# A two-layer mixer step on one core: only the first layer's shift and scale ahead of the tokens, the other modulation rows by VectorE in the merge

## The chip, the core and the metric

The kernel runs on one core of one Trainium2 chip. The metric is the device time of one launch in microseconds (us), lower is better. Engines are named as the profile names them: PE is TensorE (PEld its weight loads), DVE is VectorE, ACT is ScalarE, POOL is GpSimd, SP is SyncE. ACTq, DVEq and SPq are the sequencers of these engines; a DMA is issued from one of them.

## The reference, cut to what matters

Two layers, 1,152 tokens (1,024 latent, 128 context), model width 1,024, float32. What the change touches is the modulation:

```python
for l in range(DEPTH):                                   # DEPTH = 2
    mod = jax.nn.silu(cond) @ ada_w[l] + ada_b[l]        # (1024) @ (1024, 3072), for c and for c_ctx
    shift, scale, gate = jnp.split(mod, 3, axis=-1)
    h = rms_norm(x, norm_g) * (1.0 + scale) + shift      # needed at the start of the layer
    ...                                                  # h @ w_in, three branches
    merged = g0 * (y_a @ w_br_a) + g1 * (y_b @ w_br_b) + g2 * (y_c @ w_br_c)
    x = x + gate * (merged @ w_out)                      # gate is needed at the end of the layer
```

Latent tokens are modulated by `c`, context tokens by `c_ctx`, so each modulation row of 128 channels has two columns.

## The kernel before, in words

Channels lie on the 128 partitions: 1,024 channels are KD = 8 slices k, tokens are the free axis, cut in NT = 3 tiles of 384 columns. Every engine has a program of its own, written out by hand, and semaphores join them; no scheduler reorders anything. A projection (`product`, `tile`, `project`, L336 to L355) multiplies each float32 weight block of 128x1024 as three products (high by high, low by high, high by low), so one block over the three tiles is 8 x 3 x 3 = 72 matmuls. The result tiles rotate over PSUM banks 0, 1 and 2 (`take`, L328): a tile waits until the tile three places earlier has been read out. SP loads the weight blocks into two slots (L670, L672), POOL splits each into high and low (L686, L688) once PE is done with the block two places earlier.

**Prologue.** ACT issues `par`, `sq_c`, `mask_in`, the whole of `X` (L694 to L697) and six of the sixteen slabs of `ada_w` (L735; one slab is 128 input channels of one layer by all 3,072 outputs). ACT squares the 8 slices of X (L709) and DVE adds them up (`norm_add`, L1224, L1226), in turns through two buffers. PE sums over the partitions (`norm_sum`, L374, L377), ACT makes 1/rms (`root`, L701, L703) and then `cond` = SiLU of c (L727). Then PE makes the modulation of both layers: for each of the 16 slabs six matmuls with `cond` as the stationary operand and 512 columns moving (L393), 96 a layer; ACT copies the finished 2x3072 row block (L733, L738), PE turns it by 24 small transposes (L400), and DVE adds the bias and forms `mod` and `amul` (L1273 to L1279). ACT still works out two exponentials (L741, L743), DVE the small constants behind them (L1247 to L1268).

**First normalised slices.** For each k, DVE scales X by 1/rms into `n_t` (L1289), ACT applies scale and shift (L752) and rounds to `h_hi` (L757), DVE forms the remainder `h_lo` (L1295). PE runs the first projection slice by slice behind them (`project_as_split`, L357).

**Merge and output.** A layer ends with three merges, one a branch, of 8 rows j. For each j PE projects G(j) (72 matmuls) and Y(j) (36 matmuls); ACT takes the sigmoid of the three tiles of G (`merge`, L1127), DVE multiplies them with the tiles of Y (L1588) and adds them to X (L1592). Then come the loads of `x_res` (L1198), the split of X (L1201, L1635), and the output projection, whose read-out uses the gate rows of `mod` (L1646). Layer 1 starts with another `norm_sum`.

```python
for l in range(DEPTH):          # PE, prologue
    for k in range(KD):
        for n in range(6):
            mm = pe.matmul(ps[0:2, n, :], cond[:, k, :], slabs[:, s % 6, n * 512:(n + 1) * 512], ...)
```

## Time and profile before

| | us |
|---|---|
| median of 3 runs (3261.82 to 3265.61) | 3263.72 |
| the profiled execution, whole | 3263.88 |
| its span in the profile | 3262.0 |
| PE busy | 3102.9 (95%) |
| DVE busy | 1341.8 (41%) |
| ACT busy | 1073.5 (33%) |
| POOL busy | 696.4 (21%) |

The profile is of one execution. Its span runs from the first to the last instruction that it shows; the execution took 1.9 us more. The chain of waits is followed back from the last instruction, at each step to what released it; its pieces have a start, a length and a name. In a timeline a row is a start, a busy time and an instruction, "x4" after it means four instructions merged in that row, and the bracket at its end is the idle time before it and who ended it. A group of matmuls is pipelined: the ends are modelled, so starts are what is compared.

### The profile page before, as it was taken

Reading aid. Unit: us, or ns where it says so; the run is one execution under the profiler, and the core shown is the slowest. Engines: PE = TensorE matmul, PEld = TensorE weight load, DVE = VectorE, ACT = ScalarE, POOL = GpSimd, SP = SyncE. Lnnn points to the kernel's source line nnn. Section 1 sums busy time; section 2 is a strip of 40 time slices with the busy share of each in tenths; the row PEclk is TensorE's granted clock in tenths of the full one; section 3 lists DMA queues with packets and bytes.
Section 4 is the critical chain, followed back from the end, with each engine's and each line's share of the span. In section 5 each row is a group of like instructions: output and inputs, shape, how many; then the busy total and the mean of one; then the engine's idle time right before and its main releaser. Section 6 shows DMA issues by size and latency. Waiting matters only on the chain.

```text
span 3262.0 us, 43857 instructions
## 1 busy us (share of the span) xinstructions
PE 3102.9 (95%) x18496; PEld 2953.9 (91%) x18496; DVE 1341.8 (41%) x1777; ACT 1073.5 (33%) x2038; POOL 696.4 (21%) x404
## 2 busy tenths in 40 slices
PE   5799999999999999999988999989999999999999
PEld 1299998889889999999988999988888999999999
DVE  1255666566654111121225566646565421112121
ACT  1234344465554211010114343445565431101010
POOL 0021211111111123333331211211111112233322
PEclk9899999999999999999999999999999999999999
DMA  8310111100011012111330111110000101121131
GB/s 321 142 35 30 41 40 47 33 24 23 30 36 68 24 43 68 46 42 40 135 126 28 36 38 36 34 47 23 30 29 30 68 31 34 48 68 44 44 108 71
DMA packets 52115, 182.58 MB, mean 56 GB/s; under 512 B 5584, under 2 KB 12752, under 8 KB 49232
## 3 DMA queue, kind: packets, MB, share of 16 engines
q1 hardware_dynamic: 28800, 92.29, 9.4%
q10 hardware_dynamic: 23120, 87.49, 7.0%
q8 instruction: 147, 2.41, 0.3%
q14 instruction: 48, 0.39, 0.0%
HBM read 149.35 MB, written 30.41 MB: 55 GB/s over the span
## 4 chain that ended last, share of the span: by engine, by line
PE 88%; DVE 4%; ACT 4%; issue 1%; ACTq 1%; DMA 1%; DVEq 1%
PE ps L339 64%; PE ps L436 4%; PE ps L544 3%; PE ps L393 3%; PE ps L518 2%; PE ps L519 2%; PE ps L531 2%; DVE stat L1502 1%; PE ps L482 1%; PE ps L602 1%; DVE b_qs L1482 1%; PE ps L474 1%; PE ps L604 1%; DVEq L1483 1%; ACT b_eb L1010 1%
## 5 line engine op out<-in xcount | busy, mean ns | idle before, releaser
L339 PE MATMUL ps<-h_hi,w_hi 128*128 128x384 f32 x3648 | 1242.6, 341 | 50.0 <-DVE h_lo L1295 27.3
L339 PE MATMUL ps<-h_hi,w_lo 128*128 128x384 f32 x3648 | 1226.2, 336 | 0.0
L339 PE MATMUL ps<-h_lo,w_hi 128*128 128x384 f32 x3648 | 1226.2, 336 | 0.0
L339 PEld LDWEIGHTS ps<-h_hi,w_hi 128*128 128x128 f32 x3648 | 690.5, 189 | 58.1 <-issue 57.0
L686 POOL CAST w_hi<-w_raw 128x1024 fp32r<-128x1024 f32 x200 | 202.0, 1010 | 2524.0 <-PE ps L339 2519.2
L339 PEld LDWEIGHTS ps<-h_hi,w_lo 128*128 128x128 f32 x3648 | 690.6, 189 | 0.9 <-issue 0.5
L339 PEld LDWEIGHTS ps<-h_lo,w_hi 128*128 128x128 f32 x3648 | 689.7, 189 | 0.0
L688 POOL TENSOR_TENSOR w_lo<-w_raw,w_hi 128x1024 fp32r<-128x1024 f32 x200 | 494.2, 2471 | 16.0
L1127 ACT ACTIVATE m_g<-ps 128x384 f32<-128x384 f32 x144 | 70.7, 492 | 763.7 <-PE ps L339 754.1
L1502 DVE TENSOR_REDUCE stat<-ps 128x1 f32<-128x1152 f32 (+1 forms) x144 | 177.8, 1235 | 237.1 <-PE ps L519 237.1
L1588 DVE TENSOR_TENSOR m_p<-ps,m_g 128x384 f32<-128x384 f32 x96 | 53.5, 558 | 476.4 <-PE ps L339 476.4
L339 PE MATMUL ps<-y_lo,w_hi 128*128 128x384 f32 x576 | 192.4, 334 | 0.0
L339 PE MATMUL ps<-y_hi,w_hi 128*128 128x384 f32 x576 | 192.4, 334 | 0.0
L339 PE MATMUL ps<-y_hi,w_lo 128*128 128x384 f32 x576 | 192.4, 334 | 0.0
L544 PEld LDWEIGHTS ps<-b_wt,b_v 128*128 128x128 f32 x1168 | 138.9, 192 | 33.5 <-ACT b_wt L1017 24.5
L544 PE MATMUL ps<-b_wt,b_v 128*128 128x128 f32 x1168 | 145.1, 277 | 17.4 <-ACT b_wt L1017 17.4
L518 PE MATMUL ps<-b_kh,b_qs 128*128 128x384 f32 (+1 forms) x400 | 146.3, 366 | 14.1 <-ACT b_eb L1010 9.0
L519 PE MATMUL ps<-b_kl,b_qs 128*128 128x384 f32 (+1 forms) x400 | 134.3, 336 | 0.0
L436 PE MATMUL ps<-a_q,a_km 128*128 128x128 f32 x1008 | 132.8, 286 | 0.0
L1588 DVE TENSOR_TENSOR X<-ps,m_g 128x384 f32<-128x384 f32 x48 | 26.8, 557 | 257.5 <-PE ps L339 257.5
L436 PEld LDWEIGHTS ps<-a_q,a_km 128*128 128x128 f32 x1008 | 127.6, 192 | 2.6 <-ACT a_km L821 1.1
L1010 ACT ACTIVATE b_ea<-ps,stat 128x1152 f32<-128x1152 f32 (+1 forms) x72 | 81.3, 1129 | 144.4 <-DVE stat L1502 144.4
(226 smaller groups left out, 3582.9 us busy)
## 6 DMA issues: line engine op xcount, KB each, us to landing
w_raw<-in_w_full SPq DMA_DIRECT2D x152, 512.0 KB, 3.5
ada_slabs<-in_ada_w ACTq DMA_DIRECT2D x16, 1536.0 KB, 7.6
w_raw<-in_w_half SPq DMA_DIRECT2D x48, 256.0 KB, 2.6
x_res<-x_keep ACTq DMA_DIRECT2D x16, 576.0 KB, 8.6
out_x_new<-X ACTq DMA_DIRECT2D x16, 576.0 KB, 2.8
X<-in_x_t ACTq DMA_DIRECT2D x1, 4608.0 KB, 17.8
x_keep<-X ACTq DMA_DIRECT2D x1, 4608.0 KB, 13.3
y_keep<-a_y ACTq DMA_DIRECT2D x8, 576.0 KB, 2.8
```

The source lines that it names most:

```text
L339: mm = pe.matmul(ps[:, bank, 0:TILE], w[:, slot, k, :], r[:, k, cols_of(t)], start=(k == 0 and i == 0), stop=(k == kt - 1 and i == 2))
L393: mm = pe.matmul(ps[0:2, n, :], cond[:, k, :], slabs[:, s % 6, n * 512:(n + 1) * 512], start=(k == 0), stop=(k == KD - 1))
L436: mm = pe.matmul(o, a_km[lev % 2][:, cs], both_ways(a_q2, c, 1 << lev), start=True, stop=True)
L518: pe.matmul(o, b_qs[:, m, i * P:(i + 1) * P], b_kh[:, m, ks], start=True, stop=False)
L519: mm = pe.matmul(o, b_qs[:, m, i * P:(i + 1) * P], b_kl[:, m, ks], start=False, stop=True)
L544: mm = pe.matmul(ps[:, 6 + ring % 2, 0:P], b_v[:, CH if i == CTX else kt, :], b_wt[:, kt, :], start=(kt == 0), stop=(kt == CH - 1 or i == ...
L686: pool.tensor_copy(w_hi[:, slot, 0:kt, :], raw).then_inc(w_hi_done, 1)
L688: pool.tensor_tensor(w_lo[:, slot, 0:kt, :], raw, w_hi[:, slot, 0:kt, :].bitcast(F32), ALU.subtract).then_inc(w_split, 1)
L1010: act.activation(dst, src, ACT.Exp, bias=stat[:, pos % 3, m:m + 1], accum_out=stat[:, pos % 3, 2 + m:3 + m]).then_inc(b_exp, 1)
L1127: act.activation(m_g[:, t, :], seen(l, ("G", br, j), t), ACT.Sigmoid)\
L1502: dve.tensor_reduce(stat[:, pos % 3, m:m + 1], src, AX.X if ctx_block else AX.XY, ALU.max, negate=True).then_inc(b_max, 1)
L1588: dve.tensor_tensor(dst, seen(l, name, t), m_g[:, t, :], ALU.mult).then_inc(free(l, name, t), 1)
```

## The change

The first layer's shift and scale are worked out in four column groups; a group q holds shift rows 2q, 2q+1 and scale rows 2q, 2q+1, so that it completes slices 2q and 2q+1 of the tokens. Its weights come as two halves of 1,024 KB. ACT issues groups 0 and 1, then works out `cond`, then issues the 8 slices of X with a semaphore each, then groups 2 and 3, then the masks. SP holds the first weight block back until the last slice of X has landed. The scaled X is written in place, so DVE no longer waits for ACT's buffers (`first_scaled`, `first_affine`, `first_low`). The store of X into `x_keep` ahead of layer 0 is gone (the residual of layer 0 is read from the input), and layer 0 stores X to `x_keep` alone.

The 32 other rows (8 gate rows of layer 0, all 24 of layer 1) move to the last merge of a layer: 24 in layer 0, 8 in layer 1. ACT loads one row's weights at a time (128x1024, 512 KB, three buffers) and `cond` as 128x2x1024; DVE forms each of the two columns of a row by one `tensor_tensor_reduce` over 1,024 elements, whose product goes to PSUM banks 3 to 6 and whose sum, with the bias as its start value, goes to `mod`. `PHASES` says how many rows are summed ahead of the products of each j.

```diff
+GROUPS = 4
+LATE = ([(0, 2 * KD + j) for j in range(KD)] + [(1, j) for j in range(2 * KD)],
+        [(1, 2 * KD + j) for j in range(KD)])
+PHASES = ((0, 3, 4, 4, 4, 3, 3, 3), (0, 2, 1, 1, 1, 1, 1, 1))
+SLABS = 3
...
         @block.tensor
...
-            pe.wait_ge(const_in, 48)
-            norm_sum(0)
-            pe.wait_ge(n_rs_s, NT)
-            pe.wait_ge(cond_ready, 1)
-            for l in range(DEPTH):
...
+            def modulation_rows(q):
                 for k in range(KD):
+                    if k % 4 == 0:
+                        pe.wait_ge(group_in[2 * q + k // 4], 16)
+                    mm = pe.matmul(ps[0:2, 3 + q, :], cond[:, k, :], groups[q][:, k, :],
+                                   start=(k == 0), stop=(k == KD - 1))
+                mm.then_inc(ada_mm, 1)
...
+            pe.wait_ge(const_in, 32)
+            pe.wait_ge(cond_ready, 1)
+            modulation_rows(0)
+            modulation_rows(1)
+            modulation_turned(0)
+            norm_sum(0)
+            modulation_turned(1)
+            modulation_rows(2)
+            modulation_rows(3)
+            modulation_turned(2)
+            modulation_turned(3)
+            pe.wait_ge(n_rs_s, NT)
...
         @block.sync
         def _(sp):
+            sp.wait_ge(x_in_s[KD - 1], 16)
...
         @block.scalar
...
+            for i in range(GROUPS):
+                group_load(i)
+            act.wait_ge(const_in, 32)
+            act.activation(cond[:, :, :].rearrange("p k c -> p (k c)"), par[:, PC_C:PC_C + 2 * KD],
+                           ACT.Silu).then_inc(cond_ready, 1)
+            for k in range(KD):
+                act.dma_start(X[:, k, :], x_in[:, k, :]).then_inc(x_in_s[k], 16)
+            for i in range(GROUPS, 2 * GROUPS):
+                group_load(i)
+            act.dma_start(mask_in[:, :, :], masks).then_inc(mask_in_s, 16)
...
+            def first_affine():
+                for k in range(KD):
+                    act.wait_ge(n_xr, k + 1)
+                    if k % 2 == 0:
+                        act.wait_ge(mod_ready, k // 2 + 1)
...
+                        if last and j == 0 and t == 0:
+                            act.wait_ge(y_lo_s, l * 12 + 12)
+                            act.dma_start(cond_b[:, :, :], cond_rows).then_inc(cond_in, 16)
+                            late_load(SLABS)
+                        if last and j and t < 2:
+                            late_load(begun + SLABS + min(1 + t, PHASES[l][j]))
...
         @block.vector
...
+            row_kept(0)
+            row_kept(1)
+            modulation(0)
+            dve.wait_ge(n_rs_s, NT)
+            first_scaled(0)
+            first_scaled(1)
+            modulation(1)
+            for k in range(2, KD):
+                first_scaled(k)
+            first_low(0)
+            row_kept(2)
+            first_low(1)
+            row_kept(3)
+            modulation(2)
+            modulation(3)
+            for k in range(2, KD):
+                first_low(k)
...
+            def late_sums(l, j):
...
+                    for c in range(2):
+                        ins = dve.tensor_tensor_reduce(
+                            ps[:, 3 + 2 * c:5 + 2 * c, :], late[n % SLABS][:, :].rearrange("p (b k) -> p b k", b=2),
+                            cond_b[:, c, :].rearrange("p (b k) -> p b k", b=2), 1.0,
+                            par[:, PC_AB + layer * 24 + row:PC_AB + layer * 24 + row + 1],
+                            ALU.mult, ALU.add, mod[:, layer, row, c:c + 1])
+                    ins.then_inc(late_used, 1)
...
             def merge(l, order, br):
                 for j in range(KD):
+                    if order == len(BRANCHES) - 1:
+                        late_sums(l, j)
                     dve.wait_ge(m_gate, l * 24 + order * 8 + j + 1)
```

`row_kept(q)` is DVE's copy of a finished 2x512 row block out of PSUM, `modulation(q)` three small DVE operations that make the shift and scale of two slices.

PE's program at the start, of before (L374 and L377 are `norm_sum`, L393 the modulation matmuls, L400 the transposes, L339 the first projection):

```order
L374 MATMUL ps<-n_acc,sq_c 128x384 [waits n_added,const_in]
L377 MATMUL ps<-n_sq,sq_c 128x384 [waits n_squares]
L393 MATMUL ps<-ada_slabs,cond 2x512 [waits slab_in0,cond_ready,n_rstd]
L400 MATMUL ps<-sq_c,mod_row 128x2 [waits ada_row]
L393 MATMUL ps<-ada_slabs,cond 2x512 [waits slab_in2,ada_row]
L400 MATMUL ps<-sq_c,mod_row 128x2 [waits setup_done,ada_row]
L339 MATMUL ps<-h_hi,w_hi 128x384 [waits n_lo,n_hi,w_split]
```

and of the change (L404 the modulation matmuls of a group, L411 its transposes, L394 and L397 `norm_sum`, L358 the projection):

```order
L404 MATMUL ps<-ada_group_136,cond 2x512 [waits group_in0,cond_ready,const_in]
L404 MATMUL ps<-ada_group_137,cond 2x512 [waits group_in2]
L411 MATMUL ps<-sq_c,mod_row 128x2 [waits ada_row]
L394 MATMUL ps<-n_acc,sq_c 128x384 [waits n_added]
L397 MATMUL ps<-n_sq,sq_c 128x384 [waits n_squares]
L404 MATMUL ps<-ada_group_138,cond 2x512 [waits group_in4]
L404 MATMUL ps<-ada_group_139,cond 2x512 [waits group_in6]
L358 MATMUL ps<-h_hi,w_hi 128x384 [waits n_hi,n_lo,w_split,n_rstd]
```

The two full blocks of modulation matmuls between the norm's sums and the projection are replaced by four groups, two of them ahead of the sums; one set of transposes stands ahead of `norm_sum`, one behind it and two ahead of the projection.

DVE's program between the norm's sums and the last slice, of the change (L1339 is `row_kept`, L1347 to L1351 `modulation`, L1355 `first_scaled`, L1359 `first_low`):

```order
L1293 TENSOR_TENSOR n_acc<-n_acc,n_sq 128x1152 [waits n_squares] x6
L1339 COPY mod_row<-ps 2x512 [waits ada_mm] x2
L1347 TENSOR_TENSOR amul<-ps,scale_b 128x4 [waits ada_t]
L1355 TENSOR_TENSOR X<-X,n_rs 128x1152 [waits n_rstd]
L1355 TENSOR_TENSOR X<-X,n_rs 128x1152 x6
L1359 TENSOR_TENSOR h_lo<-X,h_hi 128x1152 [waits n_hi]
L1339 COPY mod_row<-ps 2x512 [waits ada_mm]
L1351 TENSOR_TENSOR amul<-amul,par 128x4
L1359 TENSOR_TENSOR h_lo<-X,h_hi 128x1152 [waits n_hi] x6
```

Before, DVE took one scaling and one remainder in turn for each slice; now all eight scalings stand ahead of the first remainder, and the scale and shift of slices 4 to 7 behind two remainders.

DVE's program in the last merge, of the change (L1719 and L1723 are the products and the sum of the merge, L1687 the product that completes SiLU, L1696 the two instructions of one `tensor_tensor_reduce`):

```order
L1723 TENSOR_TENSOR X<-X,m_p 128x1152
L1687 TENSOR_TENSOR cond_b<-cond_b,ps 128x2048 [waits cond_sigmoid]
L1696 ISA ps,mod<-ada_late_146,cond_b,par 128x1024 [waits late_in0]
L1696 ISA mod 128x1
L1719 TENSOR_TENSOR m_p<-ps,m_g 128x384 [waits tile_done1,m_gates]
```

The sums stand between the end of one j and the first product of the next; each is a long instruction and a short one that writes the accumulated value.

## Rows read from the trace of the kernel before

**Rows 1.** The page: busy time of the engines, and the ended-last chain by engine.

```profile
PE 3102.9 (95%) x18496; PEld 2953.9 (91%) x18496; DVE 1341.8 (41%) x1777; ACT 1073.5 (33%) x2038; POOL 696.4 (21%) x404
...
PE 88%; DVE 4%; ACT 4%; issue 1%; ACTq 1%; DMA 1%; DVEq 1%
```

**Rows 2.** The chain of waits from 0 to 175 us: start, length, what.

```profile
2.13 17.84 DMA X<-in_x_t
...
21.34 2.22 ACT n_sq L709 x2
...
32.34 4.18 PE ps L374 x6
...
42.01 0.53 ACT n_rs L703
...
44.16 43.34 PE ps L393 x96
...
158.12 1.24 ACT n_h L752
...
163.69 1.24 ACT n_h L752
...
170.87 0.78 PE ps L339 x3
```

**Rows 3.** DMA, 0 to 230 us: rate in 40 slices; issues (KB, us to landing).

```profile
GB/s 222 444 438 413 427 425 430 197 0 274 299 291 306 314 321 312 75 216 310 21 0 3 0 151 412 259 1 0 0 0 51 66 0 91 3 91 0 90 4 0
...
X<-in_x_t ACTq DMA_DIRECT2D x1, 4608.0 KB, 17.8
...
sq_c<-in_squares ACTq DMA_DIRECT2D x1, 256.0 KB, 6.1
```

**Rows 4.** Timeline of the prologue: single operations of ACT and DVE.

```profile
1.65 0.45 ACTq L696 DMA_DIRECT2D mask_in<-in_masks  x1
...
20.04 1.28 ACT L709 ACT_TABLE_LOAD   x1 [20.04 <-DMA X<-in_x_t]
...
144.48 0.21 DVE L1273 TENSOR_TENSOR mod<-ps,par 128x48 f32<-128x48 f32 x1 [2.35 <-PE ps L400]
...
145.28 2.62 DVE L1289 TENSOR_TENSOR n_t<-X,n_rs 128x1152 f32<-128x1152 f32 x2
```

**Rows 5.** Timeline of PE at the first slices: two starts, and two more later.

```profile
152.18 0.52 PE L339 MATMUL ps<-h_hi,w_hi 128*128 128x384 f32 x1
...
152.50 0.52 PE L339 MATMUL ps<-h_hi,w_lo 128*128 128x384 f32 x1
...
157.22 0.33 PE L339 MATMUL ps<-h_hi,w_lo 128*128 128x384 f32 x1
...
157.39 0.33 PE L339 MATMUL ps<-h_lo,w_hi 128*128 128x384 f32 x1
```

**Rows 6.** Timeline of DVE in the last merge of layer 0.

```profile
1452.97 0.56 DVE L1588 TENSOR_TENSOR m_p<-ps,m_g 128x384 f32<-128x384 f32 x1 [6.43 <-PE ps L339]
...
1457.71 1.36 DVE L1592 TENSOR_TENSOR X<-X,m_p 128x1152 f32<-128x1152 f32 x1
1471.69 0.56 DVE L1588 TENSOR_TENSOR m_p<-ps,m_g 128x384 f32<-128x384 f32 x1 [12.61 <-PE ps L339]
...
1475.78 0.56 DVE L1588 TENSOR_TENSOR m_p<-ps,m_g 128x384 f32<-128x384 f32 x1 [1.52 <-PE ps L339]
```

**Rows 7.** Timeline of POOL there: the remainder of a full and of a half block.

```profile
1470.76 2.40 POOL L688 TENSOR_TENSOR w_lo<-w_raw,w_hi 128x1024 fp32r<-128x1024 f32 x1
...
1476.57 2.37 POOL L688 TENSOR_TENSOR w_lo<-w_raw,w_hi 128x512 fp32r<-128x512 f32 x1
```

**Rows 8.** Single lines of DVE: duration ns min/median/max, first and last start.

```profile
L1461 DVE TENSOR_TENSOR b_q<-b_qn,b_rope x8: 1224/1225/1226, 560.7 to 2421.3; 128x1024 f32<-128x1024 f32 x8
...
L1313 DVE SCALAR_TENSOR_TENSOR a_f<-a_f,oml,lbv x8: 1409/1414/3549, 188.7 to 2018.5; 128x1152 f32<-128x1152 f32 x8
```

**Rows 9.** Groups of DVE by line and shape: busy us, mean ns, idle before.

```profile
L1470 DVE TENSOR_TENSOR b_kt<-ps,b_rope 128x512 f32<-128x512 f32 x16 | 10.4, 683 | 8.6 <-PE ps L482 8.6
```

204 lines of the change are left out of this document (130 added, 74 removed).

## The prediction

> **What bounds the kernel now.** I read the page first: PE is busy for 95% of the span, and 88% of the chain that ended last is PE [rows 1]. So a change pays only where PE works on something avoidable, or waits. Next I read the chain of waits over the first 175 us [rows 2], since the change works there. X lands at 2.13 + 17.84 = 19.97; squares and their sums take from 21.34 until `norm_sum` starts at 32.34; 1/rms ends at 42.54; then come two blocks of 96 modulation matmuls, the first of 43.34 us. Only at 170.87 does PE start the last slice of the first projection; from there the program is the same in both kernels until the last merge. This instant is my yardstick for the front. The reader should see that some 87 us of modulation are PE work in the chain that nothing else covers, and that the rest of the front is hand-over between DMA, ACT and DVE. Last I read one row j of the last merge of layer 0 [rows 6, 7], since the displaced work goes there.
>
> **The front, step by step (times in the new kernel).** It loses 192 matmuls and 48 transposes and gets 32 matmuls and 16 transposes; I follow the new chain.
>
> 1. `sq_c` lands 6.1 us after its issue near 1.2 [rows 3], so the constants are there at 7.3 and `cond` (a 128x16 activation, 0.2) at 7.5. ACT then issues 13 DMAs (8 of X, 4 half groups, the masks) at 0.45 each [rows 4]: 13.4. A table load of 1.28 [rows 4] and two tiny exponentials: about 15.1.
> 2. Is X there? Ahead of its slice 0 stand 0.6 MB of constants and 4.2 MB of groups; with slice 0 it is 5.4 MB, with all of X (4,608 KB, [rows 3]) 9.5 MB. The slices of the rate are 5.75 us long; summed up they move 5.4 MB by 15.1 and 9.5 MB by 24.9 [rows 3]. Before, X itself was complete when 7.5 MB had moved, about 0.8 MB more than stood up to its end, because later transfers share. I add 1.2 us for that: slice 0 at 16.3, slice 6 at 24.7, slice 7 at 26.1.
> 3. From the first square to the start of `norm_sum` it took 32.34 - 21.34 = 11.0 [rows 2]. From 16.3 that gives 27.3, and slice 6 with its square (1.16) and its sum (1.36) gives 27.2: both limits agree. DVE's dozen small constants of 0.2 each [rows 4] are done by 17.5, beside the first two squares.
> 4. New in the chain: PE turns group 0 ahead of `norm_sum`, and this waits for DVE's copy `row_kept(0)`, which in program order stands behind the sums. A read of 512 PSUM columns is 0.68 [rows 9], four transposes with hand-overs 0.5: 28.5. `norm_sum` to 1/rms takes 42.54 - 32.34 = 10.2 as before [rows 2]: 38.7. Groups 0 and 1 are done long before (16 matmuls from 7.5, under 1 us each); groups 2 and 3 run behind `norm_sum`, beside ACT's and DVE's work.
> 5. From 38.7 two chains race. ACT starts slice 0 after the first scaling (1.36), at 40.1, and takes (163.69 - 158.12) / 2 = 2.79 a slice [rows 2]; it wants shift and scale of slice 4 at 51.2. DVE first has eight scalings and two remainders at 1.31 (two took 2.62 [rows 4]), 13.1; two row copies at 0.68; `modulation(1)` and `(2)` at 0.8 each (from 144.48 to 145.28 [rows 4]): 16.1 in all, 54.8. **So ACT stalls for 3.6 us at slice 4**: that is what is late next in the front.
> 6. ACT takes slices 4 and 5 in 5.6, and from the start of slice 6 to PE's last slice it is 170.87 - 163.69 = 7.2 [rows 2]: 67.6. PE leaves its last transposes at about 55 with most slices waiting: nine matmuls each, 0.32 apart at the low clock level (1.2 GHz) and 0.17 apart at the high one [rows 5]. It starts low after idling, as before, so 2.9 + 6 x 1.55 bring it to about 67 too. Both meet at slice 7.
>
> Gain of the front: 170.87 - 67.6 = **103.3 us**. The weight blocks, held back until slice 7 of X, are loaded and split (3.5 us each) by about 40: hidden until 55. The dropped store of X ahead of layer 0 and the 8 dropped stores to the output ran beside PE: nothing.
>
> **The merge.** A row j lasts 1471.69 - 1452.97 = 18.7 us of PE. DVE is free from 1459.1, when its sum ends, to 1471.69, the next product: 12.6 us. PE is held only if Y(j, 0) has not been read when G(j+1, 0) wants its bank, 4.1 us later (where the third product starts, 1475.78) [rows 6]. So the room is 16 us. One sum is a DVE pass over two SBUF operands of 1,024 float32 and a short instruction; no row shows this operation. The nearest row, same operands and length, has 1.23; the longest two-operand pass has 3.55 [rows 8]. These are my bounds; I take 1.4, near the first, for the short instruction on top. Four rows of weights a j: 11.2 us. Beside it, POOL: the remainder of a half block takes 2.37, that of a full one 2.40 [rows 7], and the half one began while DVE's sum was running: it waited. I add 1.0 for DVE waiting in turn: 12.2 of 16 us, **hidden**. j = 1 has three rows and the SiLU product of 2,048 columns (2.4): 11.8, hidden. If the cover is gone, PE waits by what exceeds 16. POOL's next full split has PE's 6.2 us of Y(j) for its 3.5. ACT's new issues and waits stand behind its sigmoids, whose banks are wanted 8 us later. The 13.6 MB of new loads over 150 us are 91 GB/s, a fifth of what the prologue's stream reached. Layer 1 has one or two rows a j. I put the merge at 0, up to 3 us in this case.
>
> The Trainium skill (SBUF — State Buffer, "Who interferes with whom") has a VectorE instruction with two SBUF inputs and a GpSimd one that reads SBUF block each other for the whole instruction. By that rule the trace agrees: POOL's 2.37 us for half a block and DVE's 3.55 against a median of 1.41.
>
> **Sum.** 3263.88 (the profiled execution) - 103.3 = 3160.6. That execution lies 0.16 above the median of the runs, so I predict **3160.4 us**. For this case alone 3155 to 3166: below, X without the 1.2 us and less stall at slice 4; above, later transfers and the merge's 3 us.
>
> **Rivals.**
> - *The sums run at half rate.* At 1.2 ns an element [rows 8] doubled, 1,024 take 2.4 us. A row j lasts 1.0 + 2n x 2.4 + 3.3 (three products, sum, gaps): 23.5 for n = 4, +4.8 in three rows; 21.1 at j = 1 with the SiLU product, +2.4; n = 3 just fits. In all +17: 3177. Against: L1313 with two SBUF operands takes 1.41 for 1,152 elements [rows 8]. For: the new instruction also accumulates, and no row does. 12%. The Trainium skill (Vector Engine (DVE) Microarchitecture Reference, "Points that are easy to get wrong") states that a scalar-tensor-tensor form with two SBUF sources other than bf16 halves throughput; the row of L1313 does not show it.
> - *Each sum takes 3.5 us*, held or slow [rows 8]. n = 4: 32.3 a row, +13.6 three times; n = 3: +6.6 three times; j = 1 +9; layer 1 +2. In all +72: 3232. Against: POOL reads for 5 of 18.7 us, mostly at the row's end. 8%.
> - *Slower than before.* The same place further on: by this formula 48 sums in layer 0 and j = 1 of layer 1 stretch the merges by 52c - 110.5 for a price c, which eats 103.3 at c = 4.1 us. At 4.3 the time is 3273. No pass of this size takes that long in the trace. 2%.
> - *The front gains less.* The transfers run at 300 GB/s, as those of the later slabs did [rows 3]: slice 6 lands at 31.8 and the sums end 7 us later, 3167. Or PE stays at the low level through the first eight slices, 8 x 2.9 from 55: +9, 3169. Against: the later slabs were issued one at a time, and PE rose after 3 us before. 10%.
> - *The displaced rows stay in the prologue too* would take the gain; PE's program excludes it, with 32 modulation matmuls in all.
>
> **How the numbers follow.** Forecast 68%, half rate 12%, front less 10%, 3.5 us 8%, slower 2%. The range holds the forecast, the smaller front and the half rate: 3155 to 3177. About 0.2% (6.5 us) is what a measurement of this kernel can tell from no change. All cases but the last are faster by far more: faster 97%, same 1% (a price just above 4), slower 2%.
>
> **What would show it.** In the profile of the changed kernel: the first `n_sq` near 16, the last `n_acc` ending near 27, 1/rms near 39, ACT idle for some 3 us ahead of slice 4, PE's last slice near 67.6, no idle PE in the last merges, a sum near 1.4, products of Y right behind PE. Wrong would be: a sum above 2.0 us (PE then waits for DVE in three rows), a first square after 20, or PE waiting for `w_hi` or `w_lo` in the merge.

## The result and the profile after

| | before | after |
|---|---|---|
| median of the runs | 3264.66 (4 runs, 3261.82 to 3266.22) | 3162.8 (4 runs, 3159.06 to 3165.62) |
| profiled execution, whole | 3263.88 | 3163.95 |
| its span | 3262.0 | 3161.9 |
| start of PE's last slice of the first projection | 170.87 | 71.60 |
| the rest of the span from there | 3091.1 | 3090.3 |

The ratio is 0.969 (95% interval 0.9676 to 0.9705), 101.9 us between the medians. 3160.4 had been forecast, with 3155 to 3177 as the range. Of the 99.9 us between the profiled executions, 99.3 lie ahead of the start of PE's last slice. The rest of the kernel, with the 64 sums in its merges, lasts as long as before.

The page of the changed kernel, against [rows 1]: PE has 59 us less to do, and its share of the chain stays 88%; ACTq has gone from 1% to 2%.

```profile
PE 3043.5 (96%) x18336; PEld 2941.6 (93%) x18336; DVE 1440.4 (46%) x1920; ACT 1069.6 (34%) x2036; POOL 698.7 (22%) x404
...
PE 88%; DVE 4%; ACT 3%; ACTq 2%; issue 1%; DVEq 1%; DMA 0%
```

PE loses 59.4 us of work, but the front loses 99. Before, 102.7 us passed from the end of 1/rms (42.54) to DVE's first scaling (145.28): 86.3 in the two blocks of modulation matmuls (43.34 and 43.00), and 16.4 in the copies, the small transposes, the exponentials and the small constants around them. Now the first scaling follows 1/rms at once (44.12), since the 28 us of modulation matmuls that are left stand beside other work, half while X lands and half beside 1/rms and the first slices. Of the 102.7 us, 1.6 are given back because 1/rms ends later (44.10), and 1.9 because it now takes 27.5 us from the first scaling to PE's last slice where it took 25.6. That leaves the 99.3.

The front of the changed kernel, timeline of ACT (start, busy time, what; the bracket is the idle time before and who ended it), against [rows 2, 4]:

```profile
1.62 1.94 ACTq L725 DMA_DIRECT2D ada_group<-in_ada_first  x4
4.52 0.98 ACTq L733 DMA_DIRECT2D X<-in_x_t  x2
5.53 6.28 ACTq L733 DMA_DIRECT2D X<-in_x_t  x6
11.84 7.01 ACTq L725 DMA_DIRECT2D ada_group<-in_ada_first  x4
18.88 1.20 ACTq L736 DMA_DIRECT2D mask_in<-in_masks  x1
...
21.40 0.22 ACT L760 ACTIVATE lbt<-lbt 128x16 f32<-128x16 f32 x1
21.62 2.20 ACT L748 ACTIVATE n_sq<-X 128x1152 f32<-128x1152 f32 x2
```

The first four loads take 0.45 to 0.48 us each to issue and the first six of X 0.34 to 0.66. Then the last two of X take 4.1 us together, the four late half groups 7.01 and the masks 1.20. The chain of waits stands on them up to 20.08 and shows the single ones:

```profile
7.21 0.45 ACTq L733
7.69 1.97 ACTq L733
9.69 2.12 ACTq L733
11.84 1.98 ACTq L725
...
15.55 3.30 ACTq L725
```

ACT computes nothing in that time: it stands in the issue of a DMA for up to 3.30 us where 0.45 was expected, and the exponentials and all squares are behind it in its program. X is no longer what is waited for: its slice 0 landed at 18.15 and its slice 7 at 28.15.

Further down the chain of waits of the front: the last sum ends at 33.53, `norm_sum` runs from 34.94, and the two waits behind it are those that had been forecast.

```profile
32.17 1.36 DVE n_acc L1293
33.62 0.69 DVE mod_row L1339
34.35 0.58 PE ps L411 x4
34.94 3.89 PE ps L394 x6
38.83 1.95 PE ps L397 x6
```

Timeline of ACT and PE, the stall at slice 4 and PE's last slice (against the last row of [rows 2]):

```profile
58.94 1.63 ACT L776 ACTIVATE X<-X,mod,amul 128x1024 f32<-128x1024 f32 x2 [2.01 <-DVE amul L1351]
...
71.60 0.41 PE L358 MATMUL ps<-h_hi,w_hi 128*128 128x384 f32 x1
```

The last merge of layer 0, against [rows 6, 7]. First the two instructions of a sum, for all 64 (duration in ns min/median/max, first and last start), then DVE's timeline of row j = 2, whose four rows of the modulation are four times two sums: its first two sums and the next product; and POOL's operation at the time of the first:

```profile
L1696 DVE CUSTOM_DVE_ANT_0 ps<-ada_late,cond_b,par x64: 1282/1292/2059, 1359.7 to 3035.2; 128x1024 f32<-128x1024 f32 x64
L1696 DVE DVE_READ_ACCUMULATOR2_ANT mod<- x64: 133/140/144, 1360.9 to 3036.4; 128x1 f32 x64
```

```profile
1376.06 2.03 DVE L1696 CUSTOM_DVE_ANT_0 ps<-ada_late,cond_b,par 128x1024 f32<-128x1024 f32 x1 [0.21 <-issue]
...
1378.01 1.28 DVE L1696 CUSTOM_DVE_ANT_0 ps<-ada_late,cond_b,par 128x1024 f32<-128x1024 f32 x1
...
1388.47 0.56 DVE L1719 TENSOR_TENSOR m_p<-ps,m_g 128x384 f32<-128x384 f32 x1 [1.04 <-PE ps L358]
```

```profile
1374.63 2.37 POOL L714 TENSOR_TENSOR w_lo<-w_raw,w_hi 128x512 fp32r<-128x512 f32 x1
```

A sum starts 1.34 us after the one before it (two take 2.69), DVE is done 1.04 us before PE brings the next product, and the one sum that meets POOL's remainder takes 2.03 instead of 1.29. The two other rows of four: j = 4 has 1.04 us left too, j = 3 has nothing. There one sum waited 0.69 for its weights to land, the last one met POOL's next split (2.06), and the product of Y started at 1407.34 with no idle time ahead of it. j = 1, with three rows and the SiLU product, has 2.08 left, and the later rows of three over 3. From one addition to X to the next it is 18.72 us in every row of this merge and of layer 1's, as it was before. PE's busy time over the merge's 150 us (windows view: length, then busy time and count by engine):

```profile
1335.00:1485.00 150.00, 150.00 (x867) 150.00 (x867) 99.41 (x135) 17.92 (x29) 54.00 (x32) 1.00 0.43 136
```

So two things are to be explained by experiment: why a front whose squares started 5.3 us later than forecast ended only 4.0 late, and what the merge would have cost with dearer sums.

### The profile page after: what moved, and what is told of

It is laid out like the page before. It is cut to its first block, busy times and chain, and to the rows that moved or that the text cites. A ratio compares the mean times of both kernels' runs of the same rounds, so it can differ in the third digit from the quotient of the medians.

```text
span 3161.9 us, 43735 instructions
## 1 busy us (share of the span) xinstructions
PE 3043.5 (96%) x18336; PEld 2941.6 (93%) x18336; DVE 1440.4 (46%) x1920; ACT 1069.6 (34%) x2036; POOL 698.7 (22%) x404
## 4 chain that ended last, share of the span: by engine, by line
PE 88%; DVE 4%; ACT 3%; ACTq 2%; issue 1%; DVEq 1%; DMA 0%
PE ps L358 66%; PE ps L460 4%; PE ps L568 4%; PE ps L542 2%; PE ps L543 2%; PE ps L555 2%; DVE stat L1603 1%; PE ps L626 1%; PE ps L506 1%; DVE b_qs L1583 1%; PE ps L498 1%; PE ps L628 1%; DVEq L1584 1%; ACT b_eb L1048 1%; PE ps L476 1%
## 5 line engine op out<-in xcount | busy, mean ns | idle before, releaser
L358 PE MATMUL ps<-h_hi,w_hi 128*128 128x384 f32 x3648 | 1242.8, 341 | 35.8 <-DVE h_lo L1396 14.7
L358 PE MATMUL ps<-h_hi,w_lo 128*128 128x384 f32 x3648 | 1226.5, 336 | 0.0
L358 PE MATMUL ps<-h_lo,w_hi 128*128 128x384 f32 x3648 | 1226.2, 336 | 0.0
L358 PEld LDWEIGHTS ps<-h_hi,w_hi 128*128 128x128 f32 x3648 | 690.8, 189 | 42.6 <-issue 41.4
L358 PEld LDWEIGHTS ps<-h_hi,w_lo 128*128 128x128 f32 x3648 | 691.0, 189 | 1.0 <-issue 0.5
L358 PEld LDWEIGHTS ps<-h_lo,w_hi 128*128 128x128 f32 x3648 | 690.0, 189 | 0.0
L1719 DVE TENSOR_TENSOR m_p<-ps,m_g 128x384 f32<-128x384 f32 x96 | 53.5, 558 | 373.9 <-PE ps L358 373.9
L358 PE MATMUL ps<-y_lo,w_hi 128*128 128x384 f32 x576 | 192.4, 334 | 0.0
L358 PE MATMUL ps<-y_hi,w_hi 128*128 128x384 f32 x576 | 192.4, 334 | 0.0
L358 PE MATMUL ps<-y_hi,w_lo 128*128 128x384 f32 x576 | 192.4, 334 | 0.0
L568 PEld LDWEIGHTS ps<-b_wt,b_v 128*128 128x128 f32 x1168 | 138.9, 192 | 33.5 <-ACT b_wt L1055 24.5
L1719 DVE TENSOR_TENSOR X<-ps,m_g 128x384 f32<-128x384 f32 x48 | 26.8, 558 | 257.5 <-PE ps L358 257.5
```

The lines of the kernel that those rows point to most:

```text
L358: mm = pe.matmul(ps[:, bank, 0:TILE], w[:, slot, k, :], r[:, k, cols_of(t)], start=(k == 0 and i == 0), stop=(k == kt - 1 and i == 2))
L568: mm = pe.matmul(ps[:, 6 + ring % 2, 0:P], b_v[:, CH if i == CTX else kt, :], b_wt[:, kt, :], start=(kt == 0), stop=(kt == CH - 1 or i == ...
L1719: dve.tensor_tensor(dst, seen(l, name, t), m_g[:, t, :], ALU.mult).then_inc(free(l, name, t), 1)
```

## The experiments

Each was run once with a profile unless medians are given. "Last slice" is the start of PE's last slice of the first projection, "rest" the span behind it. Of each run's lines some stand here, the others are told.

### 1. The later groups issued by SP

**Theory A**: the front is one chain through ACT's issues, X, the sums and 1/rms, so what keeps ACT out of the issues is gained. **Rivals**: X itself lands too late, whoever issues the rest, or the hold is passed on to SP and the first weights come too late for PE.

```diff
         def _(sp):
+            sp.wait_ge(x_in_s[3], 16)
+            for i in range(GROUPS, 2 * GROUPS):
+                q, part = i // 2, slice(4 * (i % 2), 4 * (i % 2) + 4)
+                sp.dma_start(groups[q][:, part, :], ada_first[q, :, part, :]).then_inc(group_in[i], 16)
+            sp.dma_start(mask_in[:, :, :], masks).then_inc(mask_in_s, 16)
             sp.wait_ge(x_in_s[KD - 1], 16)
...
-            for i in range(GROUPS, 2 * GROUPS):
-                group_load(i)
-            act.dma_start(mask_in[:, :, :], masks).then_inc(mask_in_s, 16)
```

> Edit: the loads of groups 2 and 3 and of the masks are issued by SP, once slice 3 of X has landed, and not by ACT. Yardstick: the start of PE's last slice of the first projection, 71.60 us in the changed kernel. Theory A (the front came out 4 us later than forecast because ACT was held in issuing DMAs until 20.08, so that the exponentials, DVE's constants and the first square came late): ACT is free for its table load near 12, DVE's constants are done before X lands, the first square starts when slice 0 lands (near 18), the last n_acc ends near 29 to 30, and the last slice starts near 67.5. Theory B (X itself lands too late, whoever issues the rest): the first square moves, but the last n_acc stays above 32, since slice 6 lands late; last slice at 70 or later. Theory C (the hold is passed on: SP is held and the first weight blocks come too late): PE waits for w_hi at the first slice.

Measured: 3163.85 us, last slice 71.14, a gain of half a microsecond. Yet the front was far ahead at first. Timelines of ACT, DVE and POOL:

```profile
15.90 1.16 ACT L750 ACTIVATE n_sq<-X 128x1152 f32<-128x1152 f32 x1 [4.79 <-DMA X<-in_x_t]
...
58.10 1.63 ACT L778 ACTIVATE X<-X,mod,amul 128x1024 f32<-128x1024 f32 x2 [7.91 <-DVE amul L1353]
```

```profile
25.92 1.36 DVE L1295 TENSOR_TENSOR n_acc<-n_acc,n_sq 128x1152 f32<-128x1152 f32 x1 [0.30 <-ACT n_sq L750]
...
41.26 2.03 DVE L1353 TENSOR_TENSOR amul<-amul,par 128x4 f32<-128x4 f32 x1
```

```profile
38.09 1.74 POOL L717 CAST w_hi<-w_raw 128x1024 fp32r<-128x1024 f32 x1 [37.65 <-DMA w_raw<-in_w_full]
39.91 3.35 POOL L719 TENSOR_TENSOR w_lo<-w_raw,w_hi 128x1024 fp32r<-128x1024 f32 x1
43.21 2.24 POOL L717 CAST w_hi<-w_raw 128x1024 fp32r<-128x1024 f32 x1
```

The first square starts at 15.90 (16.3 had been forecast), the last sum ends at 27.3 (27.3) and 1/rms at 37.5, 6.6 us ahead of the changed kernel. Then the gain is lost again: SP's weight blocks come later behind the groups (the first split starts at 38.09, in the changed kernel at 35.98), POOL splits them at 38 to 49 just as DVE scales X, and both wait for each other: a 128x4 operation takes 2.03 instead of 0.16, a scaling pair 3.47 instead of 2.63, and ACT stalls for 7.91. So Theory A holds up to 1/rms, and neither rival does: X was in time, and PE waited for no weights at its first slice. What took the gain behind 1/rms is a third limit, which no expectation had named and which the trace of the changed kernel doesn't show.

Not all of the 6.6 us are the edit's. In this execution the first half group, which both kernels issue at 1.62, landed at 6.93, in that of the changed kernel at 9.26, and all that follows hangs on it (experiment 7). Some 4.2 us are left for the edit.

### 2. The same, with the first weights ahead of the groups

To tell the collision from a limit of its own, SP loads the first two weight blocks as soon as slice 3 of X has landed, and the groups behind them.

```diff
+                    if n == 0:
+                        sp.wait_ge(x_in_s[3], 16)
+                    if n == 2:
+                        for g in range(GROUPS, 2 * GROUPS):
+                            ...
```

> Edit: as e1_groups_by_sp (groups 2 and 3 and the masks by SP), but SP loads the first two weight blocks ahead of the groups, once slice 3 of X has landed. In e1 the 1/rms was ready at 37.5 instead of 44.1, and still PE's last slice started at 71.14: DVE's first scalings took 3.47 for two and 10.61 for six, beside POOL's splits of the first two weight blocks from 38.1 to 48.9. Theory A (DVE's scalings, with two SBUF operands, and POOL's splits block each other, and the late weights brought them together): the splits are over before 35, the eight scalings take 1.3 each, the last slice starts near 66 to 67. Theory B (the collision moves to the sums of squares instead, which have two SBUF operands as well): the last n_acc ends 3 us or more later than e1's 27.3 and the last slice starts at 69 or later. Theory C (the six scalings were slow for another reason, such as ACT reading X beside them): they stay slow, last slice near 71.

Measured: 3156.76 us, last slice **66.51**, rest 3088.4. POOL's first splits now lie at 28.60 to 35.50, beside `norm_sum`. Of DVE's program only one instruction meets them:

```profile
28.85 1.28 DVE L1342 COPY mod_row<-ps 2x512 f32<-2x512 f32 x2
30.14 0.16 DVE L1350 TENSOR_TENSOR amul<-ps,scale_b 128x4 f32<-128x4 f32 x1
...
30.45 1.65 DVE L1354 TENSOR_TENSOR amul<-amul,par 128x4 f32<-128x4 f32 x1
...
39.05 2.63 DVE L1358 TENSOR_TENSOR X<-X,n_rs 128x1152 f32<-128x1152 f32 x2 [6.94 <-ACT n_rs L745]
```

Theory A is shown with this: with the issues off ACT and POOL kept out of the way, 1/rms ends at 39.0 and the last slice starts 5.1 us earlier (71.60 - 66.51), 0.7 of them because the first half group landed earlier (8.59). The rivals fail: the eight scalings take 1.3 us each, and the last sum ends at 28.8, 1.5 us later than in experiment 1, whose loads had landed 1.7 earlier. The rows say more: beside the same POOL operation the copy out of PSUM and the addition with one operand in PSUM keep their 0.6 and 0.16 us, and the product of two operands in SBUF, of the same size, is held until POOL is done. The Trainium skill (SBUF — State Buffer, "Who interferes with whom") states that a VectorE instruction with two SBUF inputs contends with a GpSimd one that reads SBUF, and one with at most one such input does not; these rows agree with it.

### 3. The exponentials first, and X in one load

Two attempts at the same hold from ACT's side. In the first the two exponentials stand ahead of the later groups' issues, so that behind them only squares are left:

```diff
+            act.preload_act_table_set("natural_log_exp_and_others")
+            act.wait_ge(lb_sub, 1)
+            act.activation(lbt[:, 0:2, :, :], lbt[:, 0:2, :, :], ACT.Exp).then_inc(lb_exp, 1)
+            act.wait_ge(lam_dot, 1)
+            act.activation(lams[:, :, :], lams[:, :, :], ACT.Exp).then_inc(lam_exp, 1)
             for k in range(KD):
                 act.dma_start(X[:, k, :], x_in[:, k, :]).then_inc(x_in_s[k], 16)
```

> Edit: ACT loads the second table and works out its two small exponentials ahead of the issues of X; nothing else. Theory A (DVE's constants behind the exponentials are 2.4 us of the chain, the held issues the rest): ACT still issues until about 21.5, the first square starts there, but DVE takes it up at once: the last n_acc ends near 31.5 instead of 33.53 and PE's last slice starts near 69.5 instead of 71.60. Theory B (the landing of X bounds the sums): less than 1 us of gain.

Measured: 3160.98 us. The first square starts at 20.36 and 1/rms ends at 41.5, 2.6 earlier, but the last slice starts at 71.37, 0.2 earlier. Up to the last sum (31.2, 31.5 expected) Theory A holds; at the last slice the gain is as small as its rival's, and not by X: the first two scalings meet POOL's remainder (4.32 us for the pair, 2.63 in the changed kernel; POOL's 2.35 from 41.04), and PE, which had stood idle for 3.42 us ahead of its last transposes, is then behind, at the low clock level (granted 0.50) from 56 to 62.8.

In the second run X is one load of 4,608 KB in place of eight of 576 KB:

```diff
-            for k in range(KD):
-                act.dma_start(X[:, k, :], x_in[:, k, :]).then_inc(x_in_s[k], 16)
+            act.dma_start(X[:, :, :], x_in[:, :, :]).then_inc(x_in_s[0], 16)
```

> Edit: ACT issues X as one DMA of 4,608 KB in the same place, not as eight of 576 KB; every square waits for all of it. In the changed kernel ACT's issues took 2 us each from the fourth of X on, while before 10 DMAs went out in 0.5 us each. Theory A (the hold comes with the number of DMAs outstanding): with 8 outstanding instead of 15, ACT is through with its issues near 9 to 10. Theory B (it comes with the bytes or descriptors outstanding): ACT still issues until 16 to 20. In both the first square waits for X, near 26, the last n_acc ends near 37, and PE's last slice starts near 75, 3 to 4 us later than with slices.

Measured: 3169.43 us, last slice 79.98, 8.4 later than the changed kernel where 3 to 4 had been expected. Timeline of ACT:

```profile
4.86 2.35 ACTq L725 DMA_DIRECT2D ada_group<-in_ada_first  x4
7.24 0.45 ACTq L735 DMA_DIRECT2D mask_in<-in_masks  x1
...
27.84 3.27 ACT L747 ACTIVATE n_sq<-X 128x1152 f32<-128x1152 f32 x3 [18.52 <-DMA X<-in_x_t]
```

ACT is not held at all: its issues are over at 7.7, and the same 14.1 MB went over its queue. So **it is not the bytes that hold an issue**. What fits all traces is the number of loads that stand open on ACT's queue, issued and not landed, when the next is issued:

| run | longest issue with at most nine open | first issue with ten open: start, length |
|---|---|---|
| before | 0.79 | none, at most eight open |
| changed kernel | 0.66 | 7.69, 1.97 |
| the same again | 1.03 | 7.99, 1.30 |
| groups by SP | 0.46 | 7.72, 1.75 |
| weights first | 0.69 | 7.69, 1.30 |
| exponentials first | 0.59 | 8.88, 0.93 |
| X in one load | 0.73 | none, at most nine open |

So it is in all fourteen traces: no issue that met at most nine open loads took over 1.03 us, and each of the 29 that met ten took 0.93 to 2.12. With eleven open it is 1.2 or, once in each of the seven runs that get there, 0.5 to 0.7, and with twelve 3.1 to 3.3. A hold ends with the landings and not after a time of its own: in the seven runs with all 19 loads on ACT the last issue ends 10.8 to 10.9 us behind the landing of the first half group, also where the issues of X began 1.4 us later (exponentials first). These numbers are read off issues and landings; no run varied the count by itself. Every load of this prologue has 144 packets, whatever its size (up to 45 us ACT's queue carried 1,728 packets here, with 12 loads, and 2,736 in the changed kernel, with 19), so loads and packets can't be told apart. The prediction took its price from a prologue in which at most eight stood open.

The slices of X are worth their hold: without them the squares start at 27.84, and then POOL's splits (from 35.65) fall on the last sums: the six sums take 11.24 us together and not 8.61.

### 4. The order of the modulation in PE's program, undone

```diff
+            norm_sum(0)
             modulation_rows(0)
             modulation_rows(1)
             modulation_turned(0)
-            norm_sum(0)
```

(and DVE's `row_kept(0)`, `row_kept(1)`, `modulation(0)` behind the first scalings.)

> Edit: undoes the order alone. PE makes norm_sum first and groups 0 and 1 behind it; DVE copies and turns them after the first two scalings. Theory A (having two groups done ahead of the tokens is worth what 16 matmuls cost beyond the 1/rms, at the low clock level at which groups 2 and 3 ran, 0.87 us each): the last n_acc and norm_sum come 1.3 us earlier, but slice 0 of ACT starts near 55 instead of 45.5 and PE's last slice near 81, 9 to 10 us later. Rival (the matmuls run at the high level after norm_sum, 0.43 each, and DVE's own work up to slice 4 covers them): 1 to 4 us later.

Measured: 3174.82 us, last slice 83.14, 11.5 later. Timeline of PE:

```profile
40.40 13.89 PE L404 MATMUL ps<-ada_group,cond 128*2 128x512 f32 x32
...
55.40 13.89 PE L404 MATMUL ps<-ada_group,cond 128*2 128x512 f32 x32
```

"x32" are 16 matmuls: the trace has two records for one of this form. They take 13.9 us, 0.87 each, with the granted clock at 1.00 throughout. So 0.87 is their price at the high level; the expectation had put it down to the low one, and the rival's 0.43 is the distance of two records, not of two matmuls. Only one of the two blocks finds cover behind `norm_sum`; ahead of it, while X lands, the other costs the chain nothing. Of the 99.3 us of the front, 11.5 come from working out the first half of the groups while X lands.

### 5. The scalings spread over the chain

The changed kernel's DVE scales six slices before it copies the rows of groups 2 and 3, so ACT stalls at slice 4. Here some scalings and remainders come later:

```diff
-            for k in range(2, KD):
-                first_scaled(k)
+            first_scaled(2)
+            first_scaled(3)
+            row_kept(2)
+            first_scaled(4)
+            first_scaled(5)
+            first_scaled(6)
             first_low(0)
-            row_kept(2)
-            first_low(1)
+            modulation(2)
             row_kept(3)
-            modulation(2)
+            first_scaled(7)
             modulation(3)
-            for k in range(2, KD):
+            for k in range(1, KD):
                 first_low(k)
```

> Edit: DVE's order alone. It copies the rows of group 2 after the fourth scaling and forms shift and scale of slices 4 and 5 after the seventh, ahead of the eighth. Theory A (ACT's stall of 2.0 us at slice 4, waiting for DVE's modulation(2), is lost time in the chain): ACT runs through slices 3, 4, 5 without an idle stretch and PE's last slice starts near 69.6 instead of 71.60. Rival (PE, which started the first slices at the low level only at 58.9, is itself the bound): no more than 0.5 us.

Measured: 3162.51 us, last slice 68.38, waiting for nothing but `h_lo`; the stall at slice 4 is gone and 0.38 at slice 2 is what is left. Of the 3.2 us, 1.1 are not this edit's: 1/rms ended at 43.0 here, since the first half group had landed 0.9 earlier (8.36). So the stall of 2.01 was worth its full length, 2.1 us. The whole time fell by 1.4 only, since the rest was 3092.2 where the changed kernel had 3090.3.

### 6. The sums in the merge: none, and twice as many

Without the sums `mod` gets its bias alone (the 64 products of `cond` and `ada_w` are left out; the loads stay):

```diff
-                        ins = dve.tensor_tensor_reduce(
-                            ...
+                        ins = dve.tensor_copy(mod[:, layer, row, c:c + 1],
+                                              par[:, PC_AB + layer * 24 + row:PC_AB + layer * 24 + row + 1])
```

> Leaves out the 64 sums of the late rows: mod gets their bias alone, by copies of 128x1; the loads, the SiLU and all waits stay. Theory A (the sums are hidden): the time from PE's last first-projection slice to the end stays within 2 us of the changed kernel's 3090.3, the spread of what the other kernels show. Rival (their blocking of POOL costs PE something in each row): 3 us or more less.

Measured: 3161.21 us, last slice 71.88, rest 3087.5, which is 2.8 less than the changed kernel's 3090.3, and Theory A had allowed 2. But experiment 3, which keeps all sums, has 3087.6 and 3087.4, and the rows settle it: without the sums it is 18.72 us from one addition to X to the next in every row of these merges, exactly as with them. So the sums cost nothing, and the 2.8 us lie elsewhere (experiment 7).

Twice as many (each sum once more, with the same result) shows how much room there was:

```diff
-                    for c in range(2):
+                    for again, c in enumerate((0, 1, 0, 1)):
```

> Edit: each late sum is worked out twice in a row, 128 in all. Tests the room of 16 us a row of the merge. One row then takes 4 x 1.21 + 0.27 = 5.1 instead of 2.7. Theory A (DVE has 16 us, PE waits for what exceeds it; a merge row lasts 0.75 for POOL + n x 5.1 + 3.4): 24.6 us for n = 4, +5.8 three times; 19.5 for n = 3, +0.8 three times; 21.8 at j = 1, +3.1; in all +23 us, near 3187, PE idle on DVE in L358 in layer 0's last merge alone. Rival 1 (the banks give more room than I count): under +12. Rival 2 (late sums also make late the loads behind them, which ACT issues between its sigmoids): above +30.

Measured: 3209.24 us, rest **3135.3: 45 more**, where 23 had been expected. Timeline of DVE: four rows' sums are 16, and such a row j now takes 28.0 us (between the two additions to X, 1378.51 and 1406.53). The four rows of three take 24.6, 21.6, 23.6 and 25.5; together the seven stretch by 48 us, of which the rest of the kernel gives 3 back.

```profile
1367.91 3.40 DVE L1698 CUSTOM_DVE_ANT_0 ps<-ada_late,cond_b,par 128x1024 f32<-128x1024 f32 x1
...
1378.51 1.36 DVE L1725 TENSOR_TENSOR X<-X,m_p 128x1152 f32<-128x1152 f32 x1
...
1395.20 3.42 DVE L1698 CUSTOM_DVE_ANT_0 ps<-ada_late,cond_b,par 128x1024 f32<-128x1024 f32 x1
...
1406.53 1.36 DVE L1725 TENSOR_TENSOR X<-X,m_p 128x1152 f32<-128x1152 f32 x1
```

By the prediction's formula, 1.0 + 2n x 2.69 + 3.3, a row of four takes 25.8. In the row shown the sums that meet POOL's splits lose 3.7 us together (3.42, 2.28 and 1.80 in place of 1.29) where the formula has 1.0, and every row has one that meets the split of a full block (3.17 to 3.42). While DVE idled at a row's end, most of POOL's full split fell into its idle time; once it doesn't, each row pays for it. The expectation's second rival, weights that come late, had the number (over 30), but no sum waited for its weights in this run.

### 7. The parts put together

All of 1 to 5 that gained: groups by SP behind the first weights, the exponentials first, the scalings spread; and the changed kernel again, timed beside it. And the same with the weights behind the groups, as the collision's counter-test.

> The changed kernel once more, in rounds beside the kernel before, so that the last run stands against it on the same chip. Both theories: 3,160 to 3,166 us, about 0.969 of before, PE's last slice of the first projection starts near 71.6 us, and ACT's issues end near 20 us.

> The three edits together: the last four column groups and the masks issued by SP (with the first late weights ahead of them), the exps ahead of the waits for X, and the scalings of slices 3 to 7 spread over the merge. Theory A (the front is one chain, and each of the three took its own piece out of it): ACT free of issues at 9.5, exps over by 11, last n_acc ends at 27 to 29, 1/rms at 37.5 to 39.0, ACT's slices without a stall over 0.5 us, PE's last slice starts at 62.5 to 64.5 (66.5 with the weights first, less a stall of 2.3 and up to 1.5 more), total 3,152 to 3,155, which is 0.997 of the changed kernel. Rival (POOL's splits and VectorE's scalings collide again wherever both move, so the pieces don't add): a scaling that takes over 1.5 us behind 1/rms, last slice at 66 to 68, total 3,156 to 3,159.

> As the run of all three, but the weight blocks come behind the groups on SP's queue, as in the first run of groups by SP. Theory A with its collision: POOL's splits of the late blocks lie at 38 to 48 us beside VectorE's scalings behind 1/rms, one of which then takes over 2 us, ACT stalls over 2 us once, last slice at 67 to 70, some 4 to 6 us behind the run of all three. Rival (the place of the weights does not matter, the exps and the spread scalings were what was missing): last slice within 1.5 us of the run of all three.

| | median (runs) | last slice | 1/rms ends | rest |
|---|---|---|---|---|
| changed kernel again | 3162.05 (5) | 71.98 | 44.5 | 3087.6 |
| all three | 3159.48 (4) | 66.14 | 41.1 | 3095.1 |
| the same, weights late | 3162.57 (1) | 70.31 | 39.4 | 3090.4 |

The counter-test came out as Theory A has it: with the weights late the first pair of scalings takes 5.46 us and ACT stalls for 3.24 at slice 4, and 1/rms at 39.4 is worth less than 1/rms at 41.1 without the collision, by 4.2 us at the last slice. But all three together reached 66.14 and not 62.5 to 64.5, and the time fell by 2.6 us only (ratio to before 0.9677, 0.9664 to 0.969, beside 0.9687, 0.9674 to 0.970: not told apart). The number is the one that the rival had, its mechanism is not: no scaling took over 1.37 us. ACT's timeline with all three shows what the front now waits for:

```profile
6.87 5.30 ACTq L744 DMA_DIRECT2D X<-in_x_t  x6
18.60 1.16 ACT L756 ACTIVATE n_sq<-X 128x1152 f32<-128x1152 f32 x1 [11.82 <-DMA X<-in_x_t]
```

With the groups gone from ACT the squares wait for X anyway, so the exponentials ahead of it can gain nothing. That they delay its loads, and so cost something, was the theory of one more run, which undoes that part.

> Groups 2 and 3 and the masks by SP with the first weights ahead of them, and the scalings spread; the exps stay behind the issues of X. Theory A (moving the exps ahead delayed the issues of X by 1.0 us and with them the front): last issue of X near 11.2, X slice 7 squared from 28.9, 1/rms at 39, ACT without a stall, PE's last slice at 63.7 to 64.3. Rival (X's landing scatters from run to run by a microsecond or two, the exps had no part): last slice at 65.5 to 66.5. On the rest of the kernel: in the ten runs so far, span less the start of the last slice went with the PE clock lost in short low stretches behind the front (29.9 to 42.7 us lost, rest 3,087.4 to 3,095.1, about 0.6 a lost us). If that holds, this run's rest is 3,068.7 + 0.6 x its lost clock, within 1 us; if the longer rest of the run of all three came from its front, the rest here is 3,094 to 3,096 at any clock. Median: Theory A 3,154 to 3,158, the rival 3,158 to 3,161.

Measured: median 3158.70 of 5 runs (3156.3 to 3160.57), ratio to before 0.9677 (0.9664 to 0.9691). ACT's issues of X end at 10.85 and the last square starts at 28.58 (28.9 expected), ACT has no stall, and the last slice starts at 64.93, 0.6 later than Theory A's bound and 0.6 earlier than the rival's; the median is in the rival's range. ACT's first square is now

```profile
17.25 1.16 ACT L756 ACTIVATE n_sq<-X 128x1152 f32<-128x1152 f32 x1 [4.76 <-DMA X<-in_x_t]
```

The landings decide, and for the rival:

| run | X's first issue | first half group lands | slice 0 of X lands |
|---|---|---|---|
| changed kernel | 4.52 | 9.26 | 18.15 |
| the same again | 4.30 | 8.80 | 17.69 |
| groups by SP | 4.46 | 6.93 | 15.81 |
| weights first | 4.39 | 8.59 | 17.45 |
| exponentials first | 5.89 | 9.39 | 18.29 |
| all three | 5.87 | 9.60 | 18.51 |
| the same, weights late | 5.81 | 8.10 | 16.93 |
| last run | 4.22 | 8.27 | 17.16 |

Slice 0 lands 8.8 to 8.9 us behind the first half group in all twelve runs that load X in slices, whether X was issued at 4.2 or at 5.9. So where the exponentials stand has no part in it. What scatters, by 2.7 us between executions, is the landing of the first half group, which stands ahead of X and is issued at 1.62 or 1.63 in every run. The run of all three had it 1.3 us later than this one, and its last slice came 1.2 later: the two are alike.

Against experiment 2 the last slice should come 2.3 us earlier by the stall that is gone and 0.3 by the loads, at 63.9. What is missing is `norm_sum`, which took 6.8 us here (29.75 to 36.5) and 5.6 in experiment 2 (30.04 to 35.7). The windows view at that time (window, length, then busy time and count by engine, granted clock, DMA share, GB/s), first of experiment 2, then of this run:

```profile
29.00:31.00 2.00, 1.41 (x6) 1.10 (x7) 1.91 (x5) 1.08 (x1) 1.92 (x2) 0.67 0.96 399
...
33.00:35.00 2.00, 2.00 (x7) 1.17 (x7) 0.00 (x0) 0.00 (x0) 1.92 (x2) 0.97 1.00 418
```

```profile
29.00:31.00 2.00, 1.76 (x6) 1.33 (x7) 1.85 (x5) 0.74 (x1) 1.92 (x2) 0.50 1.00 416
...
33.00:35.00 2.00, 2.00 (x4) 1.01 (x3) 0.00 (x0) 0.00 (x0) 1.92 (x2) 0.50 1.00 418
```

The granted clock, the third number from the end, stood at the lower of its two levels (0.50, 1.2 of 2.4 GHz) through all of `norm_sum` here and through two thirds of it there. PE had been idle ahead of both. The edits between the two touch neither, so I put this 1.1 us down to the execution: the changed kernel's own two profiles differ by 0.8 there (5.9 and 6.7).

**Where the rest's 3087 to 3095 us come from.** In windows of 5 us over the whole kernel the granted clock drops in short stretches at ten to fourteen places of the program, much the same in each run, but not equally long. Two of these places in the changed kernel's second run, then in the run of all three (same view):

```profile
490.00:495.00 5.00, 2.91 (x14) 2.62 (x13) 1.53 (x2) 4.66 (x9) 3.45 (x2) 0.86 0.01 2
495.00:500.00 5.00, 2.75 (x14) 2.42 (x13) 4.38 (x4) 4.78 (x7) 0.00 (x0) 0.80 0.48 129
```

```profile
490.00:495.00 5.00, 2.23 (x10) 1.76 (x10) 4.54 (x4) 4.78 (x6) 0.47 (x1) 0.50 0.41 131
495.00:500.00 5.00, 5.00 (x16) 5.00 (x17) 3.27 (x3) 1.05 (x3) 0.00 (x0) 0.50 0.00 0
```

PE had waited 2.1 to 2.8 us for ACT's issues (ACTq L868 and L1012 in the changed kernel) at these places. I added up (1 - granted clock) x 5 us over all windows behind the front that are below 0.97 (the one that reaches past the end of the span counts whole):

| run | lost clock, us | rest |
|---|---|---|
| without the sums | 29.9 | 3087.5 |
| changed kernel again | 31.8 | 3087.6 |
| weights first | 35.9 | 3088.4 |
| changed kernel | 37.1 | 3090.3 |
| last run | 37.7 | 3091.9 |
| scalings spread | 38.5 | 3092.2 |
| all three | 42.7 | 3095.1 |

The last run was a test of this: 3,068.7 + 0.6 x 37.7 = 3091.3 was to come and 3091.9 came. Over the twelve runs with no more than 64 sums the correlation is 0.92, 0.6 us of rest to a lost one. Two executions of one and the same kernel differ by 5.3 in it and by 2.7 in the rest, so much of it belongs to the execution. That the lost clock is the cause of the longer rest is argued from this, no run sets it. Whether the front's timing moves it too, the runs don't tell. This scatter is why the edits of the last run, which bring PE's last slice 6.7 us forward (71.60 to 64.93), show only 3.4 us between the medians (3162.05 and 3158.70), with intervals that overlap: no version here is shown to beat the changed kernel.

## Why the prediction was right, and where it was not

The mechanism was right: the modulation left the chain, and the merge hid the sums. The instant that was forecast for the yardstick was 67.6, measured was 71.60; of the gain 103.3 became 99.3. But a first square after 20 had been named as a sign of being wrong, and it came (21.62): step 1 of the front failed, and the total stayed close because other terms went the other way. Point by point:

1. **ACT's issues (step 1) were mis-sized.** 13 DMAs at 0.45 each, 5.9 us, took 15.6 (4.52 to 20.08), up to 3.30 each. The price came from a prologue in which no issue met more than eight open loads [rows 4]; here the last seven met ten to twelve. The constants landed at 4.5 and not at 7.3, so the issues began 3 us early; it made no difference, since they end with the landings (experiment 3). The exponentials were over at 21.6 and not at 15.1. Experiments 1 and 2 show that this is the term: with the groups taken off ACT, 1/rms ends 4.2 to 4.4 us earlier beyond what the loads' own scatter gives.
2. **X (step 2) was forecast 2 us too early**, which the changed kernel hides behind step 1: slice 0 landed at 18.15 (16.3 forecast), slice 6 at 26.73 (24.7) and slice 7 at 28.15 (26.1). Over the runs with slices slice 0 came between 15.81 and 18.51; that experiment 1 met the forecast is the luck of one execution. So of the 5.3 us by which the squares were late, X alone would have made 1.9.
3. **The sums (step 3)** took 11.9 from the first square to their end and not 11.0. The small constants had been put beside the first two squares; they now wait for the late exponentials, and the chain passes through them from 21.65 to 24.0 before the first sum. The last sum ended at 33.5 and not at 27.3.
4. **The turn and `norm_sum` (step 4).** The copy and the turn took 1.4 (1.2 forecast). From there to the end of 1/rms it took 9.2 and not 10.2, since `norm_sum` was 1.0 shorter than before. Groups 0 and 1 ran from 9.40, when the first half group had landed, to 25.84 and not from 7.5; X covered it.
5. **The stall (step 5)** stood where it had been forecast, at slice 4, for `amul` of group 2, with 2.01 us and not 3.6: DVE's work from 1/rms to there took 14.8 and not 16.1, by the pitch of its scalings (1.27 and not 1.31) and the copies (0.6). Experiment 5 shows that it was worth its length.
6. **PE and ACT meet at the last slice (step 6)**: yes, within a microsecond; in experiment 5, where ACT comes earlier, PE waits 0.43 for `h_lo`, and with the exponentials first it is PE that is late.
7. **The merge** was put at 0, and it is: 1.35 us a sum (1.4 forecast); in the three rows of four 0.74, 1.51 and 0.74 lost to POOL (1.0 forecast) and 1.04, 0 and 1.04 us of DVE left ahead of the next product; no wait of PE. The row without any idle time still lasted 18.72, as it should by the 4.1 us that the prediction grants behind the product.

So +5.3 at the start of the squares, +0.9 in the sums, +0.2 in the turn, -1.0 in `norm_sum` and -1.6 at the stall make 3.8 of the 4.0 by which the last slice was late. The profiled execution of the changed kernel is thus 3.3 above the 3160.6 of the sum (4.0 in the front, less 0.8 in the rest), and the median lies 1.2 under that execution: 2.4 above the forecast. That it is so close is in part luck: 6.4 us of delay in steps 1, 3 and 4 met 2.6 us of gain in `norm_sum` and at the stall. One and the same kernel gave 3158.5 to 3166.8 us.

One count was loose, in the kernel's description ("96 a layer") and in the prediction. The 192 matmuls that the front "loses" are records of the trace, two for each matmul of float32; they are 96 matmuls, 48 a layer, against the 32 that are left (64 records). The sum isn't touched, since it went by the length of the blocks and by "under 1 us each" (0.87).

**The rivals.** The half rate didn't come about: the sum over 1,024 elements with its read-out takes 1.34 us, and the row of L1313 [rows 8] had told this rightly. But it was priced wrongly. At +17 us, 3177 was the top of the range; experiment 6, with 2.69 us where this rival had 2.4, cost 45. By the formula 2.69 would be some +31; what it lacked is that a longer DVE phase loses its idle time, in which POOL's full split had been hidden, and both then hold each other in each row. So at half rate the time would most likely have left the range, and the cases at 3.5 us and slower were under-priced in the same way; this is argued from experiment 6, no run has these prices. The smaller front (transfers at 300 GB/s) didn't come about; the front was smaller by another cause.
